# Differential attention as one stream over its heads: long and short query tiles in turn, the next head's queries turned in the middle of a head

## What is computed

```python
    qd = _rms(q_dif.reshape(B, T, DIFF_KV_HEADS, DIFF_GROUP, 2, HEAD_DIM), w['diff_q_norm'])
    kd = _rms(dk.reshape(B, K, DIFF_KV_HEADS, 2, HEAD_DIM), w['diff_k_norm'])
    def diff_block(qp, qb):
        dist = qp[:, None] - k_pos[None, :]
        s = jnp.einsum('bqngmd,bknmd->bngmqk', qb, kd, preferred_element_type=f32) * (HEAD_DIM ** -0.5)
        s = s - slopes_b[:, :, None, None, None] * dist.astype(f32)
        p = _masked_softmax(s, dist >= 0)
        a = p[:, :, :, 0] - lam * p[:, :, :, 1]
        return jnp.einsum('bngqk,bknv->bqngv', a.astype(vd.dtype), vd)
    o_b = _rms(o_b, w['diff_subln']) * (1.0 - lam_init)
```

## Time and profile before

| what | value |
|---|---|
| median of 3 runs | 2254.08 us (2253.2 to 2257.63) |
| the profiled execution, its own time | 2250.43 us |
| its span in the profile | 2248.6 us |
| PE busy | 2054.2 us, 91% of the span |
| DVE busy | 1148.2 us, 51% |
| ACT busy | 629.9 us, 28% |
| POOL busy | 119.0 us, 5% |

### The profile page before, as it was taken

The page is one execution under the profiler, slowest core; times in us unless marked ns, Lnnn a source line. Parts: engine busy times, 40 slices in busy tenths (PEclk is TensorE's granted clock), DMA queues, the critical chain, the costliest instruction groups (busy, mean ns, idle before and its releaser), DMA issues. The chain is left out here.

```text
span 2248.6 us, 35510 instructions
## 1 busy us (share of the span) xinstructions
PE 2054.2 (91%) x12626; PEld 1829.8 (81%) x12626; DVE 1148.2 (51%) x2510; ACT 629.9 (28%) x1212; POOL 119.0 (5%) x176
## 2 busy tenths in 40 slices
PE   5989999978995999998887969789999999999997
PEld 1338889858995888887667967589999999999996
DVE  0434333323235666766877643545555555555555
ACT  2113334411222555654773011211111011011012
POOL 1031100001300000000102000000000000000000
PEclk9999999988996998998999989889999999999998
DMA  9765545212101000000002351032201211112104
GB/s 316 256 197 176 154 133 176 79 41 82 48 1 61 1 0 0 0 0 0 1 0 86 122 179 56 20 103 57 56 28 56 56 28 56 50 34 56 37 1 151
DMA packets 132511, 166.07 MB, mean 74 GB/s; under 512 B 15851, under 2 KB 98635, under 8 KB 132372
## 3 DMA queue, kind: packets, MB, share of 16 engines
q1 hardware_dynamic: 117790, 134.75, 19.0%
q0 software_dynamic: 4832, 17.15, 2.4%
q10 hardware_dynamic: 9808, 13.11, 1.7%
HBM read 144.31 MB, written 22.77 MB: 74 GB/s over the span
## 5 line engine op out<-in xcount | busy, mean ns | idle before, releaser
L1659 DVE TENSOR_TENSOR late_x<-late_x,ffn_po 128x344 f32<-128x344 f32 x528 | 244.1, 508 | 116.5 <-PE ffn_po L1589 116.3
L1572 PE MATMUL ffn_pg<-late_words_hi,ffn_uhi 128*128 128x344 f32 x528 | 169.3, 321 | 14.6 <-DVE ffn_ulo L1623 14.6
L1533 ACT ACTIVATE ffn_sg<-ffn_pg 128x344 f32<-128x344 f32 x66 | 30.2, 458 | 534.1 <-PE ffn_pg L1572 534.1
L1589 PE MATMUL ffn_po<-ffn_a_hi,ffn_ohi 128*128 128x344 f32 x528 | 169.0, 320 | 0.2 <-DVE late_x L1659 0.2
L1572 PE MATMUL ffn_pg<-late_words_lo,ffn_uhi 128*128 128x344 f32 x528 | 169.1, 320 | 0.0
L1572 PE MATMUL ffn_pg<-late_words_hi,ffn_ulo 128*128 128x344 f32 x528 | 169.1, 320 | 0.0
L1589 PE MATMUL ffn_po<-ffn_a_hi,ffn_olo 128*128 128x344 f32 x528 | 168.9, 320 | 0.0
L1572 PE MATMUL ffn_pv<-late_words_hi,ffn_uhi 128*128 128x344 f32 x528 | 168.8, 320 | 0.0
L1572 PE MATMUL ffn_pv<-late_words_lo,ffn_uhi 128*128 128x344 f32 x528 | 168.7, 319 | 0.0
L1572 PE MATMUL ffn_pv<-late_words_hi,ffn_ulo 128*128 128x344 f32 x528 | 168.7, 319 | 0.0
L1589 PE MATMUL ffn_po<-ffn_a_lo,ffn_ohi 128*128 128x344 f32 x528 | 168.2, 319 | 0.0
(11 more groups left out here) (456 smaller groups left out, 4625.9 us busy)
## 6 DMA issues: line engine op xcount, KB each, us to landing
mod_wr<-in_w_ada SPq DMA_DIRECT2D x12, 2048.0 KB, 9.1
ffn_raw_u<-in_w_ffn_in SPq DMA_DIRECT2D x44, 512.0 KB, 5.7
dec_kin<-in_cache_kv SPq DMA_DIRECT2D x64, 256.0 KB, 3.6
ffn_raw_o<-in_w_ffn_out SPq DMA_DIRECT2D x22, 512.0 KB, 3.8
gate_d<-dec_gate ACTq DMA_DIRECT2D x48, 172.0 KB, 2.3
late_x<-gate_d SPq DMA_DIRECT2D x8, 1032.0 KB, 5.6
dec_raw<-in_w_in POOLq DMA_DIRECT2D x16, 512.0 KB, 5.6
dec_vin<-in_cache_kv SPq DMA_DIRECT2D x64, 128.0 KB, 2.2
```

The costliest lines, as they stand in the source:

```text
L1533: act.activation(sg[(j + c) % 2][:], pg[(j + c) % 2][:, 0:TCH], ACT.Silu).then_inc(silu_done, 1)
L1572: mm = pe.matmul(bank[b][:, 0:TCH], w[j][:, v * KD + k, :], h[:, k, tok], start=(k == 0 and q == 0), stop=(k == KD - 1 and q == 2))
L1589: mm = pe.matmul(po[u % 4][:, 0:TCH], w[j][:, k * P:(k + 1) * P], a[j][:, tok], start=(q == 0), stop=(q == 2))
L1659: dve.tensor_tensor(total[:, k, tok], total[:, k, tok], po[u % 4][:, 0:TCH], ALU.add).then_inc(o_read, 1)
```

## The change

The four heads become one list of 32 pairs (head, tile), and the tiles of a head are taken in the order 7, 0, 6, 1, 5, 2, 4, 3. A pair is two score items. The two items for the rotation of the next head's queries stand in the list ahead of the head's fifth tile (tile 5). `qhi` and `qlo` have four buffers instead of two, so that two heads' queries can be held at once. All items, rotations too, take the two score buffers in turn. PE's loop over heads is written out. The rotation and the scaling of `tsel` after the last head are gone, and so are the semaphore `turn`, which nobody waited for, and `q_lo`. `tsel` is scaled right ahead of the first tile of each head. In the last head `mean_heads(0, 3)` stands in the sixth tile's step, the root in the seventh's and `invert_heads(0, 3)` in the eighth's.

```diff
+    TILES = [7, 0, 6, 1, 5, 2, 4, 3]
     NU = 2 * TT
-    groups = [(i + 4) // 4 for i in range(TT)]
+    pairs = [(j, k, i) for j in range(NDH) for k, i in enumerate(TILES)]
+    NPAIR = len(pairs)
+    Q_AT = 4
+
+    items = [("queries", m) for m in range(2)]
+    for p, (j, k, i) in enumerate(pairs):
+        if k == Q_AT and j + 1 < NDH:
+            items += [("queries", 2 * (j + 1) + m) for m in range(2)]
+        items += [("scores", 2 * p + m) for m in range(2)]
+    groups = [(i + 4) // 4 for j, k, i in pairs]
+    turned_up_to = np.cumsum([0] + groups).tolist()
     second = np.cumsum([0] + [n - 1 for n in groups]).tolist()
...
-        qhi = [s.sb(f"qhi{m}", [P, SEQ], F32R) for m in range(2)]
-        qlo = [s.sb(f"qlo{m}", [P, SEQ], F32R) for m in range(2)]
+        qhi = [s.sb(f"qhi{m}", [P, SEQ], F32R) for m in range(4)]
+        qlo = [s.sb(f"qlo{m}", [P, SEQ], F32R) for m in range(4)]
...
-                    pool.wait_ge(q_ps, j * 2 + 1)
+                    if j:
+                        pool.wait_ge(q_ps, 2 * j)
...
-                transpose_queries(0)
-                with pe.Fori(0, NDH // 2) as n:
-                    for gg in range(2):
-                        j = n * 2 + gg
-                        for i in range(TT + 3):
-                            if i < TT:
-                                scores(n, j, i)
-                            if i == TT:
-                                transpose_queries(j + 1)
-                            if 2 <= i < TT + 2:
-                                transpose_probs(j, i - 2)
-                            if i > 2:
...
+                for n, (kind, x) in enumerate(items):
+                    slot, m = n % 2, x % 2
+                    if n >= 2:
+                        pe.wait_ge(sc_free, n - 1)
+                    if kind == "queries":
+                        pe.wait_ge(q_dup, 2 * x + 2)
+                        for t in range(TT):
+                            mm = pe.transpose(sc[slot][:, t * P:(t + 1) * P], qd[:, t, m].rearrange("p a b -> p (a b)"), g.ident[:])
+                        mm.then_inc(q_ps, 1)
+                        continue
+                    p = x // 2
+                    j, k, i = pairs[p]
+                    if p == 0 and m == 0:
+                        pe.wait_ge(sc_free, 2)
+                    at = j % 2 * 2 + m
+                    for a, b in key_chunks((i + 1) * P):
+                        key = (j // 2 * 2 + m) * SEQ
+                        for y, q in enumerate((qhi[at], qlo[at])):
+                            mm = pe.matmul(sc[slot][:, a:b], q[:, i * P:(i + 1) * P], g.kkd[:, key + a:key + b], start=(y == 0), stop=(y == 1))
+                    mm.then_inc(sc_full, 1)
+                    if m == 1:
+                        if p >= 2:
+                            transpose_probs(p - 2)
+                        if p >= 3:
+                            values(p - 3)
+                transpose_probs(NPAIR - 2)
+                values(NPAIR - 3)
+                transpose_probs(NPAIR - 1)
+                values(NPAIR - 2)
+                values(NPAIR - 1)
...
+                for n, (kind, x) in enumerate(items):
+                    if kind == "queries":
+                        act.wait_ge(q_ps, x + 1)
+                        act.activation(qhi[x % 4][:], sc[n % 2][:], ACT.Copy).then_inc(q_hi, 1)
+                        continue
+                    p, m = x // 2, x % 2
+                    j, k, i = pairs[p]
+                    if m == 0 and p >= 2:
+                        evacuate(p - 2)
+                    act.wait_ge(biased, x + 1)
+                    pr = prob[x % 6][:, 0:(i + 1) * P]
+                    act.activation(pr, pr, ACT.Exp, bias=nmax[:, x % NU:x % NU + 1], scale=-1.0,
+                                   accum_out=total[:, x % NU:x % NU + 1]).then_inc(p_full, 1)
+                    if m == 1 and p >= 4:
+                        finish(p - 4)
+                    if m == 1 and j == NDH - 1 and k == 6:
+                        act.wait_ge(o_mean, 1)
+                        act.activation(oss[:, :, 0:j], oss[:, :, 0:j], ACT.Sqrt).then_inc(o_root, 1)
+                evacuate(NPAIR - 2)
+                finish(NPAIR - 4)
...
-                                dve.sem_inc(turn, 1)
...
+                for n, (kind, x) in enumerate(items):
+                    at_sc = sc[n % 2]
+                    if kind == "queries":
+                        dve.wait_ge(q_hi, x + 1)
+                        dve.tensor_tensor(qlo[x % 4][:], at_sc[:], f32(qhi[x % 4][:]), ALU.subtract).then_inc(sc_free, 1)
+                        continue
+                    p, m = x // 2, x % 2
+                    j, k, i = pairs[p]
+                    if k == 0 and m == 0:
+                        dve.tensor_scalar(g.tsel[:], g.tsel[:], 0.25, None, ALU.mult).then_inc(tab, 1)
+                        dve.wait_ge(tab, j + 2)
+                    dve.wait_ge(sc_full, x + 1)
+                    if p >= 3:
+                        dve.wait_ge(tp_full, turned_up_to[p - 2])
+                    dve.tensor_tensor_reduce(prob[x % 6][:, 0:(i + 1) * P], at_sc[:, 0:(i + 1) * P], g.tsel[:, SEQ - (i + 1) * P:SEQ], -1.0, 3e38,
+                                             ALU.add, ALU.min, nmax[:, x % NU:x % NU + 1]).then_inc(biased, 1)
+                    dve.wait_ge(biased, x + 1)
+                    dve.sem_inc(sc_free, 1)
+                    if m == 0:
+                        continue
+                    if j == NDH - 1 and k == 5:
+                        mean_heads(0, j)
+                    if j == NDH - 1 and k == 7:
+                        invert_heads(0, j)
+                    if p >= 1:
+                        join(p - 1)
+                    if p >= 2 and groups[p - 2] == 2:
+                        second_half(p - 2)
+                join(NPAIR - 1)
+                for v in range(NPAIR - 2, NPAIR):
+                    if groups[v] == 2:
+                        second_half(v)
...
```

More of the change, by code:

```diff
@@ L884, in diff_attention @@
         tp_full, tp_act, tp_dve = s.sem("tp_full"), s.sem("tp_act"), s.sem("tp_dve")
-        turn = s.sem("turn")
         pv_done, o_free, o_step = s.sem("pv_done"), s.sem("o_free"), s.sem("o_step")
@@ L938, in transpose_probs @@
                         mm.then_inc(tp_full, 1)
-                def values(n, j, v):
-                    nt = v + 1
-                    pe.wait_ge(o_free, j * TT + v + 1)
-                    for gr in range(groups[v]):
-                        if gr == 0:
-                            pe.wait_ge(tp_act, j * TT + v + 2)
-                        else:
-                            pe.wait_ge(tp_dve, j * NG2 + second[v] + 2)
-                        for q in range(4 * gr, min(nt, 4 * gr + 4)):
-                            mm = pe.matmul(out[v % 2][:], probT[v % 2][:, q, :],
-                                           g.z[:, q, ds(n * 2 * HD + C_DV, 2 * HD)], start=(q == 0), stop=(q == nt - 1))
-                    mm.then_inc(pv_done, 1)
@@ L954, in scores @@
-                def scores(n, j, i):
-                    for m in range(2):
-                        pe.wait_ge(sc_free, j * (NU + 2) + 2 * i + m + 3)
-                        for a, b in key_chunks((i + 1) * P):
-                            for x, q in enumerate((qhi[m], qlo[m])):
-                                mm = pe.matmul(sc[m][:, a:b], q[:, i * P:(i + 1) * P], g.kkd[:, ds(n * 2 * SEQ + m * SEQ + a, b - a)],
-                                               start=(x == 0), stop=(x == 1))
-                        mm.then_inc(sc_full, 1)
@@ new lines, in evacuate, with finish @@
+                def evacuate(v):
+                    n = min(4, pairs[v][2] + 1)
+                    act.wait_ge(tp_full, turned_up_to[v] + 1)
+                    if v >= 2:
+                        act.wait_ge(pv_done, v - 1)
+                    act.activation(probT[v % 2][:, 0:n, :].rearrange("p a b -> p (a b)"), tp[0][:, 0:n * P],
+                                   ACT.Copy).then_inc(tp_act, 1)
+                def finish(v):
+                    j, k, i = pairs[v]
+                    act.wait_ge(pv_done, v + 1)
+                    act.activation(g.z[:, i, j * 2 * HD + C_QD:(j + 1) * 2 * HD + C_QD], out[v % 2][:], ACT.Copy, scale=share[:, i, 0:1]).then_inc(o_step, 1)
+                    act.activation(junk[v % 2][:], out[v % 2][:], ACT.Square, scale=share[:, i, 0:1],
+                                   accum_out=oss[:, i, j:j + 1]).then_inc(o_free, 1)
@@ L1021, in _ @@
+                evacuate(NPAIR - 2)
+                finish(NPAIR - 4)
+                evacuate(NPAIR - 1)
+                for v in range(NPAIR - 3, NPAIR):
+                    finish(v)
                 act.wait_ge(o_mean, 2)
```

153 lines of the change are left out of this document (41 added, 112 removed).

## The result

The changed kernel takes 2262.07 us (median of 8 runs, 2259.41 to 2262.72) against 2253.94 us for the kernel before in the same session: ratio of the means 1.0031, interval 1.002 to 1.0042. It is slower, by 8.1 us in the medians, where I had forecast +3 and "no change". The time lies in my range (2248 to 2266 us).

What follows compares the result with a forecast made beforehand. The prediction took DVE's instruction list plus its standstills to bound the stage. Its terms summed to +3.0 us: 2253.4 on the profiled execution, 2257.1 us forecast as median, counted as no change; range 2248 to 2266 us.

Steps and rivals of the forecast that it cites:

- Start: Stage start: tile 7's scores at half clock delay DVE's first pass by 1.8 us, two short waits add 0.5; +2.3.
- Head boundaries and rotation: Head ends: old waits go, -4.35 us; mid-head: DVE waits 1.25 us for `qhi` at each of three rotations, +3.75.
- My walk: Layout of DVE, PE and ACT from tile 6's first pass to the mid-head rotation; PE and ACT both ready at 6.95 us.
- The dropped semaphore: DVE's score passes: without `turn` between a tile's two passes, 0.09 us saved 32 times; -2.9 us, between 0 and -5.8.
- Long tiles behind short ones: PE's scores for a long tile after a short one just fit DVE's work; cost taken as 0.
- My margins of 0.1 to 0.3 at tile 6: Tile 6 behind tile 0: DVE has 3.0 us of work, PE needs 2.7 at full clock, so PE just fits.
- PE too late for the long tiles: Rival: at half clock PE is late for long tiles, 4.5 us a head; 2266 with half the stage low; chance 0.08.
- The prediction's own sign of being wrong: In the profile after: PE's scores often releasing DVE's passes, stage clock under 0.8, or `qlo` waiting over 2 us.
- Low clock inside heads: PE's clock within heads: short tiles no longer stand together, so less low clock; -0.4 us, between 0 and -1.
- The end: Stage end: POOL starts later and meets DVE's last joins; last copy +1.55 us, tail to next stage +2.45 us.

Runs made afterwards that it cites:

- e2: Changed kernel with the rotation of the next head's queries moved ahead of the pair's transposes and values on PE; ratio to the kernel before 1.0033.
- e10: Changed kernel with the next head's queries rotated ahead of the sixth pair of a head instead of the fifth; ratio to the kernel before 1.0046.
- e9: Changed kernel in natural tile order (0 to 7), with the rotation back at the head boundary and four query buffers kept; ratio to the kernel before 1.0011.
- e8: Kernel before with one line deleted, DVE's increment of the semaphore `turn` behind each score pass's wait; ratio to the kernel before 0.9989.
- e7: Changed kernel in natural tile order, with shares kept for each of the 32 pairs; 2253.65 us, ratio to the kernel before 0.9997.
- e4: Changed kernel with shares kept per pair (32 slots instead of 8), removing the join's wait for a free output; ratio to the kernel before 1.002.
- e1: Changed kernel with the tiles of a head in the order 0 to 7 again, the rest kept; ratio to the kernel before 0.9993.
- e5: Changed kernel with the tiles of each head in descending order, 7 to 0; ratio to the kernel before 0.9996.
- e11: Changed kernel with descending tiles, shares per pair, and mean, root and inverse of heads 0 to 2 earlier in the last head; 2252.66 us, ratio 0.9986.

## Why the prediction was off

The range held; the call of "no change" did not. That the range held owes something to luck: the stage, on which the whole sum rests, moved by 6.7 us and not by 3.0, and of the 8.1 us in the time a part lies in code that is the same in both kernels. By its own steps:

- *Start*, 1.8 ahead of the first pass and 0.5 behind it: measured +0.1 ahead. The cost of tile 7's scores was nearly as forecast: 1.4 us more behind the last `qlo` than before, 0.4 less than my term, because the first 512-column product came at the higher clock (0.47 us, and 0.56 and 0.63 from the third on). What I overlooked is the gain of 1.3 us ahead of it, 1.05 of it from the first rotation's finer wait for POOL's copies. It hid part of the real miss.
- *Head boundaries and rotation*, -4.35 + 3.75: the rotation's sum is close (4.3), but the forecast had three times 1.25 and the trace has 0.69, 1.70 and 1.89. My walk let tile 7's values begin without a wait; ahead of the two long ones they waited 0.80 and 0.99 us for ACT to free the output buffer. That PE and ACT are both critical there was right: in e2 ACT comes late by its own queue, and in e10 it goes from a finish to `qhi` without a pause. In natural order the whole move is worth about 2 us (e9), where my terms gave 0.
- *The dropped semaphore*, -2.9: right. e8 gives -3.1 in the core.
- *What I overlooked*: `join` has a new wait, on `o_free`, from the ninth pair on, though the text ahead of the prediction calls its instructions the same as before. It is always long satisfied, and still puts 0.06 us ahead of the reciprocals. By the rows that is 1.4 us for 24 waits; in natural order its removal gave 0.4 us of core (e7), and e4's 1.9 is mixed with the clock of the last head. It was in the diff, and I costed it at nothing.
- *Long tiles behind short ones*, 0: **the step that failed.** The seven late places sum to 5.9 us, or 4.1 if each is granted the ordinary gap. Two things were missing in it. The first is the clock in the place (3.5 of the 5.9). My margins of 0.1 to 0.3 at tile 6 held at full clock (no wait there in the changed kernel's first head, in e10's third and in e4's fourth) and not at half. I had asked whether the *mean* clock of the stage would be under 0.8; it was 0.94 in the core. The second is PE's wait for the output buffer (1.75 of the 5.9 stand behind it, at full clock, a part of them as an echo of a fall just before): I had counted PE's work between two scores as if nothing in it waited. So my rival "PE too late for the long tiles" had the right effect and one of its two causes, with a wrong condition and a chance of 0.08. The prediction's own sign of being wrong came up, PE's scores releasing DVE's passes often (16 times).
- *Low clock inside heads*, -0.4: the granted clock of the steady head is 0.95 in both kernels; that of the core rose from 0.92 to 0.94.
- *The end*, +1.55 and +2.45: the tail is right to 0.1, though not in the order of its steps. In the core the meetings with POOL cost 2.7 us against 1.8 before, +0.9.

In sum for the core: forecast -1.3 (with the 0.5 of the start), measured +4.1. Towards these 5.4 us late long scores bring about 4, the wait in `join` 0.4 to 1.4 and the rotation 0.6; meetings with POOL, 0.6 under my term, take some back. The parts are read from rows and not each switched off by a run: e1 and e5 show that the order is the cause and what it costs, and none of the runs changes the clock or the number of output buffers alone. A third output buffer, or the finish ahead of the exponentials in ACT's queue, would test the second cause; neither was tried. At clock 1.00 the alternating head of e10 (32.2) is still 1.3 us longer than the descending one (30.9), of which its rotation's wait, 1.25 us against 0.32, makes 0.9. Open too is why the code ahead of the stage, the same in all, takes up to 6.5 us longer in e2 and e10.

## What to carry to other kernels

Where a margin is a few tenths of a microsecond, don't test it against the mean clock but against the clock in that place. In this kernel the alternating order put the heaviest tile but one right behind the pause after which the clock fell, in three heads of four; descending order had no fall in its second and third heads.

When an engine's work between two deadlines is added up, ask of each part whether it can begin at all. Here the value products depend on a buffer that another engine frees, and that engine's queue still holds a long tile when PE's holds a short one.

And count waits that are already satisfied: on the engine that sets the pace they took 0.06 us each here.

## What the runs showed of the hardware

An increment of a semaphore by DVE between two of its passes cost 0.07 us (gap 0.33 before, 0.26 in e8), and a wait that is long satisfied 0.06 (0.15 us ahead of the reciprocal in e4, 0.21 in the changed kernel). In the first three pairs, where the pass doesn't wait for a transposed tile as well, the gap is 0.19 us, another 0.07 less.

The Trainium skill (SBUF — State Buffer, Who interferes with whom) has `tensor_scalar` among the DVE instructions that can take the pair of ports shared with GpSimd, if its operands permit. The traces agree for one of eight columns (`a_oss` 128x8). It took 0.16 us in the kernel before, when POOL was done; 0.29 in the changed kernel, ending at 1203.15 where POOL's instruction ends at 1203.13; and in e11 it ends at 1190.32, POOL's at 1190.29:

```profile
1188.73 1.59 DVE L1058 TENSOR_SCALAR a_oss<-a_oss 128x8 f32<-128x8 f32 x1 [2.63 <-ACT dif_junk L998]
```
